# Group A's probability transposes one unit later on TensorE

## The reference

```python
mod = silu(c) @ w_ada[l] + b_ada[l]                 # six rows: shift, scale, gate, twice
proj = (rms_norm(x) * (1 + sc1) + sh1) @ w_in[l]    # split into groups A, B, C, D
# A: differential attention, 4 heads, two score maps per head
p = softmax(q @ k.T * scale)                         # maps 0 and 1
a = p[0] - lam * p[1];  o = a @ v;  ya = rms_norm(o, subln_g) * (1 - lam_init)
# B: neighbourhood attention with bias   C: convolution   D: dilated attention
x = x + gt1 * (concat(ya, yb, yc, yd) @ w_out[l])
x = x + gt2 * hier_moe(...)                          # 32 experts, top-2 in the top-1 group
```

## Time and profile before

| | us |
|---|---|
| median of three runs | 2031.31 (2028.75 to 2036.29) |
| profiled execution, its own time | 2029.6 |
| its span, first to last instruction | 2027.8 |
| TensorE busy | 1671.9 (82%) |
| VectorE busy | 579.9 (29%) |
| ScalarE busy | 508.2 (25%) |
| GpSimd busy | 225.0 (11%) |
| mean granted clock of TensorE | 0.899 of full |

### The profile page before, as it was taken

One profiled execution on the slowest core, in us unless ns is written; L12 is line 12 of the kernel. 1 busy time (PEld: TensorE's weight loads), 2 busy tenths in 40 slices (PEclk: granted clock), 3 DMA queues, 4 the chain that ended last, 5 costly groups with the idle time before them and its releaser, 6 DMA issues. The chain is left out here.

```text
span 2027.8 us, 22664 instructions
## 1 busy us (share of the span) xinstructions
PE 1671.9 (82%) x7664; PEld 833.4 (41%) x7664; DVE 579.9 (29%) x1251; ACT 508.2 (25%) x1109; POOL 225.0 (11%) x223
## 2 busy tenths in 40 slices
PE   4999988898877888888849999879589788887882
PEld 2456544454333333333325655444434333333331
DVE  1373344223211111111145614541311111111114
ACT  2100644421211111111230116461121111122112
POOL 2000012010111011111030002021101111111101
PEclk7999967997989989989969999789789999899886
DMA  9423423136999889999971225230369999999994
GB/s 338 149 83 108 153 99 134 42 124 249 377 396 397 354 336 397 411 411 397 409 248 54 92 83 185 99 128 21 120 270 364 400 400 399 405 418 410 396 390 158
DMA packets 91445, 527.49 MB, mean 260 GB/s; under 512 B 13936, under 2 KB 20176, under 8 KB 66800
## 3 DMA queue, kind: packets, MB, share of 16 engines
q1 hardware_dynamic: 72720, 489.43, 61.3%
q0 software_dynamic: 13104, 24.51, 3.9%
q10 hardware_dynamic: 5552, 12.65, 1.7%
HBM read 521.04 MB, written 23.86 MB: 269 GB/s over the span
## 5 line engine op out<-in xcount | busy, mean ns | idle before, releaser
L1075 PE MATMUL ps<-ring,arena 128*64 128x512 f32 x2928 | 702.6, 639 | 160.8 <-DMA ring<-in_w_exp_up 138.3
L1075 PEld LDWEIGHTS ps<-ring,arena 128*64 128x64 f32 x2928 | 255.0, 147 | 565.2 <-issue 558.3
L811 PE MATMUL ps<-ring,hT 128*128 128x512 f32 (+1 forms) x1024 | 365.3, 515 | 6.5 <-ACT tmp L1245 4.9
L811 PEld LDWEIGHTS ps<-ring,hT 128*128 128x128 f32 x1024 | 193.5, 191 | 164.6 <-issue 147.3
L565 DVE TENSOR_TENSOR arena<-ps,arena 64x512 f32<-64x512 f32 (+1 forms) x64 | 44.4, 693 | 681.6 <-ACT arena L1344 480.3
L1344 ACT ACTIVATE arena<-ps 128x512 f32<-128x512 f32 x64 | 38.2, 597 | 613.2 <-PE ps L1075 586.4
L772 POOL DMA_INDIRECT yexp_d<-arena,masks x64 | 59.2, 925 | 921.2 <-DVE arena L573 921.2
L1336 ACT ACTIVATE arena<-ps,modc 128x128 f32<-128x128 f32 x256 | 96.2, 456 | 59.3 <-PE ps L1063 58.4
L554 DVE TENSOR_SCALAR arena<-ps,modc 128x128 f32<-128x128 f32 x256 | 87.5, 404 | 57.3 <-PE ps L1063 57.2
L1063 PE MATMUL ps<-cst,arena 128*128 128x128 f32 x512 | 77.0, 296 | 28.0 <-DMA arena<-xn_d,masks 28.0
L1063 PEld LDWEIGHTS ps<-cst,arena 128*128 128x128 f32 x512 | 64.6, 195 | 78.3 <-issue 64.9
(11 more groups left out here) (182 smaller groups left out, 1328.9 us busy)
## 6 DMA issues: line engine op xcount, KB each, us to landing
ring<-in_w_exp_gate SPq DMA_DIRECT2D x64, 2048.0 KB, 15.1
ring<-in_w_exp_up SPq DMA_DIRECT2D x64, 2048.0 KB, 18.4
ring<-in_w_exp_down SPq DMA_DIRECT2D x64, 2048.0 KB, 9.9
ring<-in_w_ada SPq DMA_DIRECT2D x24, 2048.0 KB, 9.3
ring<-in_w_in SPq DMA_DIRECT2D x8, 2048.0 KB, 22.8
ring<-in_w_out SPq DMA_DIRECT2D x4, 2048.0 KB, 8.9
ring<-in_w_in SPq DMA_DIRECT2D x6, 1024.0 KB, 12.7
xn_d<-arena ACTq DMA_DIRECT2D x8, 512.0 KB, 2.6
```

Source lines behind the costliest of these rows:

```text
L811: last = pe.matmul(out, lhs(k), rhs(k), start=(k == 0), stop=(k == n - 1))
L1075: last = [pe.matmul(outs[c][HALF * c:HALF * c + HALF, :], lhs(k)[:, 0:HALF], rhs(c, k), start=(k == 0), stop=(k == n - 1), tile_position=( ...
```

## The change

- `LAG` gives each group a distance between a unit's scores and its transposes: 2 steps for D and B as before, 3 for A. `TURN_STEP[u]` is the step in which unit u is transposed. Step 10 has no transposes; step 26 has those of unit 23 (A) and unit 24 (B).
- The output product follows one step behind the transposes, as before (`closed_at`), so it is a step later for A; step 27 has those of pairs 15 and 16. `summed_at` puts VectorE's mix of an A unit a step later as well, in step u + 2; for D and B the reciprocal stays at u + 1.
- Units of A and B use three pairs of probability buffers in turn. The third, `late_probs`, lies over V of group D; its first user, unit 10, waits for D's last output product.
- The squares of A now lie over V of A, and the norm works on them in place.
- `squares_a` moves from step 27 to 28, `MEAN_A` from steps (27, 28) to (31, 32), the logarithms and exponentials from step 28 to 32, and `subln` from step 29 to 33.
- The number of steps goes from 36 to 35; the last one had nothing in it for TensorE.

```diff
-NSTEP = NU + 4
+LAG = {"D": 2, "A": 3, "B": 2}
+TURN_STEP = [u + LAG[UNITS[u][0]] for u in range(NU)]
+NSTEP = NU + LAG["B"] + 1
-MEAN_A = (LAST_U["A"] + 4, LAST_U["A"] + 5)
+MEAN_A = (NU - 1, NU)
-def closes(u):
-
-    return 0 <= u < NU and UNITS[u][3] != 0
+def turned_at(step):
+
+    return [u for u in range(NU) if TURN_STEP[u] == step]
+
+
+def closed_at(step):
+
+    return [u for u in turned_at(step - 1) if UNITS[u][3] != 0]
+
+
+def summed_at(step):
+
+    return [u for u in range(NU) if u + LAG[UNITS[u][0]] - 1 == step]
...
-        sqA = v["D"].rearrange("p t c -> p (t c)").rearrange("p (f s) -> p f s", f=2)
-        lnA = v["A"].rearrange("p t c -> p (t c)").rearrange("p (f s) -> p f s", f=2)
+        sqA = v["A"].rearrange("p t c -> p (t c)").rearrange("p (f s) -> p f s", f=2)
+        late_probs = v["D"].rearrange("p t c -> p (t c)").rearrange("p (f s) -> p f s", f=2)
...
         def unit_probs(u):
-            return prob[2 * (u % 2)], prob[2 * (u % 2) + 1]
+            k = u % 2 if u < FIRST_U["A"] else (u - FIRST_U["A"]) % 3
+            return (late_probs[:, 0, :], late_probs[:, 1, :]) if k == 2 else (prob[2 * k], prob[2 * k + 1])
...
             if u < 2:
                 await_filled(eng, (l, "qkT", "B", TT - 1))
+            elif u == FIRST_U["A"] + 2:
+                await_filled(eng, (l, "o", PAIR_OF[LAST_U["D"]]))
             else:
-                await_filled(eng, (l, "probT", u - 2, 0 if UNITS[u - 2][0] == "A" else 1))
+                old = u - 2 if u < FIRST_U["A"] + 2 else u - 3
+                await_filled(eng, (l, "probT", old, 0 if UNITS[old][0] == "A" else 1))
...
                 for i in range(NSTEP):
-                    if 2 <= i < NU + 2:
-                        turn(i - 2)
+                    for u in turned_at(i):
+                        turn(u)
                     if i < NU:
                         scores(i)
-                    if closes(i - 3):
-                        attend(i - 3)
+                    for u in closed_at(i):
+                        attend(u)
...
                 for i in range(NSTEP + 1):
-                    if closes(i - 4):
-                        rinv_out(i - 4)
-                    if 2 <= i < NU + 2:
-                        prob_out(i - 2)
+                    for u in closed_at(i - 1):
+                        rinv_out(u)
+                    for u in turned_at(i):
+                        prob_out(u)
...
                 for i in range(NSTEP + 1):
-                    if closes(i - 4):
-                        heads_out(i - 4)
+                    for u in closed_at(i - 1):
+                        heads_out(u)
                     if i < NU:
                         maxima(i)
-                    if 1 <= i <= NU:
-                        sums_inverted(i - 1)
-                    if i == LAST_U["A"] + 4:
+                    for u in summed_at(i):
+                        sums_inverted(u)
+                    if i == TURN_STEP[LAST_U["A"]] + 2:
                         squares_a()
```

More of the change, by code:

```diff
@@ L161, in plan_banks @@
         for i in range(NSTEP):
-            if 2 <= i < NU + 2:
-                for h in range(1 if UNITS[i - 2][0] == "A" else 2):
-                    take((l, "probT", i - 2, h), "tr")
+            for u in turned_at(i):
+                for h in range(1 if UNITS[u][0] == "A" else 2):
+                    take((l, "probT", u, h), "tr")
             if i < NU:
@@ L167, in plan_banks @@
                     take((l, "score", i, c), 2 * (i % 2) + c)
-            if closes(i - 3):
-                take((l, "o", PAIR_OF[i - 3]), "o")
+            for u in closed_at(i):
+                take((l, "o", PAIR_OF[u]), "o")
         for step in range(NSTEP):
@@ L1305, in _ @@
                             await_filled(act, key)
-                            drains(act.activation(lnA[:, f, :], bank(key), ACT.Ln, bias=C["eps"]), key)
+                            drains(act.activation(sqA[:, f, :], bank(key), ACT.Ln, bias=C["eps"]), key)
                         for f in range(2):
                             await_drained(act, (l, "meanA", f))
-                            act.activation(lnA[:, f, :], lnA[:, f, :], ACT.Exp, scale=-0.5).then_inc(rootA_ready, 1)
+                            act.activation(sqA[:, f, :], sqA[:, f, :], ACT.Exp, scale=-0.5).then_inc(rootA_ready, 1)
                 for t in range(TT + 1):
@@ L1619, in subln @@
                         y = yT[:, FIRST_F["A"] + f, :]
-                        last = dve.scalar_tensor_tensor(y, y, subg[:, 0:1], lnA[:, f, :], ALU.mult, ALU.mult)
+                        last = dve.scalar_tensor_tensor(y, y, subg[:, 0:1], sqA[:, f, :], ALU.mult, ALU.mult)
                     last.then_inc(yA_ready, 1)
                 for i in range(NSTEP + 1):
-                    if closes(i - 4):
-                        heads_out(i - 4)
+                    for u in closed_at(i - 1):
+                        heads_out(u)
                     if i < NU:
                         maxima(i)
-                    if 1 <= i <= NU:
-                        sums_inverted(i - 1)
-                    if i == LAST_U["A"] + 4:
+                    for u in summed_at(i):
+                        sums_inverted(u)
+                    if i == TURN_STEP[LAST_U["A"]] + 2:
                         squares_a()
```

## The result

The changed kernel took 2056.84 us in the median of 4 runs (2050.08 to 2062.32), the one before 2031.46 (4 runs, 2028.75 to 2036.29): a ratio of 1.0118, 95% interval 1.0088 to 1.0147. It is 25 us slower. The forecast was 2051. The ratios and intervals in this document leave out three executions in which the granted clock was 0.55 to 0.73 and which took 2254, 2537 and 2909 us (one of experiment 4, one of the kernel before beside experiments 9 and 10, one of experiment 5); the medians in the table contain them.

The account below looks back on a forecast made before the run. Bound: a busy TensorE, with group A's transposes waiting for a mix queued behind VectorE's maxima. Per layer 0 + 5 - 0.6 - 2.5 + 8.1 = +10.0, both +20, so 2051 us; range 2030 to 2067.

Parts of the forecast that it names:

- The loop: Group A steps: transposes, scores, maxima, mix keep their 5.66 us period, as the mix stands behind the maxima; cost 0.
- The parity: Steps T11 to T25: output products move one step against fixed modulation products, so attend meets ada; +5 us a layer.
- full step: Group A step with attend and ada: 4.7 us at the faster clock, 8.4 at the slower; 7.0, half slow, was used.
- The gap at step 10: Step 10 has no transposes, so TensorE does less before the loop starts: -0.6 us.
- The seam and the norm: T25 to T31: seam steps grow, the norm of A leaves; 30.7 us plus 1.5 for slow clock, -2.5 a layer.
- The stall: Step 27: TensorE idles 3.6 us before the second output product, until VectorE has emptied the one output bank.
- step 25: Seam from A to B: attend beside ada, 4.8 us instead of 3.5, plus 0.75 for the mix beside GpSimd.
- The tail: T31 to output projection: the norm without cover, 17.45 us against 11.83; with slow products +8.1 us a layer.
- The allowance for the clock: Tail: 2.5 us (0 to 5) added for products and first output products running at 1.2 GHz.
- The sum: Whole kernel: +10.0 us a layer, +20 for both layers; 2049.6 us profiled, 2051 as median.
- Rival 1: Attention stage: the clock takes no part; +1 us a layer, 2033 us; chance 0.21 including results up to the forecast.
- rival 2: Group A stretch: full step always slow, tail +10; +18.4 us a layer, 2068 us; chance 0.17.

Follow-up runs that it names:

- experiment 4: The kernel before, with VectorE's mix of unit i-1 ahead of the maxima of unit i in group A: 2007.7 us, ratio 0.9877 to the kernel before.
- experiment 9: Experiment 8's kernel with the second mean product in bank 0 instead of bank 7: 2000.6 us, ratio 0.9833 to the kernel before.
- experiment 10: Experiment 9's kernel with ScalarE's norm at step 33, behind unit 29's inverse sums, and the scaling at 34: 2001.1 us, ratio 0.9844 to the kernel before.
- experiment 5: The changed kernel with a lag of 3 for group B as well, so no step has two output products: 2040.9 us, ratio 1.0020 to the kernel before.
- experiment 7: The changed kernel with the mix of group A ahead of the maxima: 2008.5 us, ratio 0.9870 to the kernel before.
- experiment 6: The changed kernel with lag 3 in group B and the modulation products one step later: 2045.4 us, ratio 1.0069 to the kernel before.
- experiment 3: The kernel before, with only the modulation products and their column forms one step later: 2047.5 us, ratio 1.0080 to the kernel before.
- experiment 1: The kernel before, with only the norm of A late (mean products at steps 31 and 32): 2030.7 us, ratio 0.9986 to the kernel before.
- experiment 8: The kernel before, with the mix of A ahead of the maxima and the norm of A late: 2002.0 us, ratio 0.9845 to the kernel before.

## Why the prediction was right

**The loop.** Right. The wait of 2.54 us is there unchanged, and line 957's waits for the mix grew to 34.9 us. Experiments 4 and 7 show that VectorE's order held it, and experiment 6 that the lag alone is neutral.

**The parity.** Predicted +5 a layer, measured +4.3 between T11 and T25; experiment 3 gives +5.3 with nothing else changed and experiment 6 takes it away. The sum for a full step that is slow throughout was 8.4; I went by a half slow one of 7.0, and the six in the trace took 7.7 in the mean (7.2 to 8.5). The attend steps without ada were shorter than I had them (4.3 to 5.2 us against 5.3 to 5.66), and the two misses nearly cancel. One reading beneath it was wrong: in layer 1 of the kernel before, the attend step was not at 2.4 GHz. Timeline of the kernel before, step 12:

```profile
1267.72 1.92 PE L967 MATMUL ps<-probsT,arena 128*64 128x128 f32 x16
```

The step that stands behind the plain step's wait ran at 1.2 GHz in its transposes, scores and attend. Before, that was the attend step, which took 5.66 us (1269.84 - 1264.18) with 0.20 us of idleness; in the changed kernel it is the fullest step, which has no idleness to hide in. The picture of a clock that is low for longer holds only in part: by twice the missing share of the clock, 49 and 38 us of A were at 1.2 GHz before, and 48 and 51 in the changed kernel (84.87 us at 0.72, 85.68 at 0.70).

**The gap at step 10.** Predicted -0.6; measured -0.2 and -0.6.

**The seam and the norm.** Predicted 32.2 for T25 to T31, measured 34.0 and 34.2. The norm's going is worth 10.7 us a layer (34.7 less experiment 1's 24.05), as my durations have it (34.7 - 24). All that the seam adds to those 24 us was 10.1 (34.1 - 24.05), where I had 8.2. Of it the double product with its clock is the largest part: without it B was 8.3 us shorter (experiment 5), with one product moved to the tail. The stall was 3.21 us, I had 3.6. The term that was short is step 25, with attend and ada: 7.6 and 7.9 us (345.12 - 337.49, 1356.61 - 1348.71), I had 5.5. In layer 0 its transposes, scores and attend ran at 1.2 GHz; in layer 1 a part of its scores and its attend did, and 1.51 us are the wait for the mix behind the coefficient's 2.08. The prediction set aside a wait for GpSimd's whole operation because a mix had not shown one; the operation in front of the mix does.

**The tail.** Predicted +8.1, measured +7.4 and +6.4. The product of unit 30 started 13.0 us after T31 in both layers, where I had 13.25, and the starts before it came within 0.3 us as well. With the product at 2.4 GHz the next one stood 2.08 us behind it in layer 1, with a slow one 3.17. The allowance for the clock was a little high.

**The sum.** +10.0 a layer predicted, +10.2 measured in the stage. That it agrees so closely is in part luck: A was put 0.7 too high and the tail 1.2, B 1.9 too low. Rival 1, without the clock, had +1, and rival 2, with the clock low throughout, +18.4; the clock's part lies between them. The profiled execution is 32.7 us longer than the one before; of the 12 us outside the two stages, 3.3 are the output projections' slow starts. The rest lies between the output projection and the next layer or the end, where executions of one kernel differ as much (four of the changed kernel spread over 12 us). What of it is the change's is left open.

By the Trainium skill's "ScalarE: Activation LUTs" (section "What ACT_TABLE_LOAD costs") the tail would have been 2.8 us longer a layer. The load is 1.28 us in the changed kernel too, with the logarithm 0.01 us behind it (377.47 + 1.28, 378.76): the trace decides against it.

## What to carry to other kernels

Before giving a wait more distance, look at what the waiting instruction is queued behind: here the mix waited for nothing but its place in VectorE's order, and moving it ahead of the maxima brought 1.2%, where a third buffer and a longer lag brought nothing. A lag of one step in part of a pipeline also moves that part's other work against everything that has a fixed beat, makes two of a thing at the seam to the next part, and takes the cover from what must follow the part; price each of the three. Work that stood as a stall in the middle can be cheaper or dearer at the end: the norm saved 10.7 us where it left and cost 6.4 where it came.

## What the runs showed of the hardware

- The granted clock of TensorE decides the price of a step's place. A step with attend and ada is 4.7 us by sum at 2.4 GHz; between T11 and T25 of the changed kernel, where each of them stood directly behind a wait of 2.5 us and its transposes, scores and attend ran at 1.2 GHz, it took 7.2 to 8.5. Behind the wait of 2.93 us in the tail sixteen products took 1.92 us at once in layer 0; in layer 1 the first sixteen still took 1.04 and the next 1.92.
- A VectorE operation on two SBUF inputs of 128x512 took 1.50 us beside GpSimd work instead of 0.75; GpSimd's kept its 2.45. The coefficient in front of it, one element wide, took 0.73 and 2.08 us instead of 0.22 and ended both times within 0.03 us of GpSimd's operation.
- Taking 1.4 us out of ScalarE's row in the tail shortened the tail by 1.4 us where the products behind ran at 1.2 GHz in both kernels, and by 0.2 where they had run at 2.4 GHz before (experiments 8 and 9).
